# Earlier sorting of x's rows, y's parts made by blocks and halves, and block numbers loaded later on VectorE

## What is computed

```python
h = hybrid_mixer(x, ...)                       # ends with merged @ w_out
x = layer_norm(DEEPNORM_ALPHA * x + h, ln1_w, ln1_b)
# hier_moe: pick one of 4 groups, then the top 2 of its 8 experts for every token
g_sel = argmax(x @ router_group_w + b);  p_group = softmax(...)[g_sel]
top_logit, top_local = lax.top_k(e_logits of that group, 2)
weight = p_group * softmax(top_logit)
order = argsort(expert ids)                    # 512 (token, expert) rows, sorted by expert
hid = silu(xb @ w_gate[e]) * (xb @ w_up[e])    # per expert, 1024 -> 256
yb = hid @ w_down[e]                           # 256 -> 1024
y = zeros.at[token].add(yb * weight)
x = layer_norm(DEEPNORM_ALPHA * x + y, ln2_w, ln2_b)
```

## Time and profile before

| | us |
|---|---|
| median of 3 runs | 1702.05 (1702.04 to 1709.67) |
| profiled execution, its own time | 1701.53 |
| its span in the trace | 1700.3 |
| TensorE products busy | 1543.8 (91%) |
| VectorE busy | 1016.6 (60%) |
| ScalarE busy | 789.8 (46%) |
| all DMA, mean | 183 GB/s |

### The profile page before, as it was taken

How to read it: one execution, slowest core, us unless ns; L and a number is a source line. 1 busy time by engine, 2 the same in 40 slices (tenths; PEclk the granted TensorE clock), 3 DMA queues, 4 the chain that set the end, 5 groups by cost and what they waited for, 6 DMA issues and landing times. The chain is left out here.

```text
span 1700.3 us, 22867 instructions
## 1 busy us (share of the span) xinstructions
PE 1543.8 (91%) x9455; PEld 1304.7 (77%) x9455; DVE 1016.6 (60%) x1264; ACT 789.8 (46%) x1143; POOL 236.5 (14%) x337
## 2 busy tenths in 40 slices
PE   4988899999988899998989898999979899999996
PEld 4977789998977789997987786677868766666664
DVE  6668676666664664445464445773333666666666
ACT  3554565455464565444532312223201476666662
POOL 6530100001340000002880002200002000000000
PEclk9998899999998899999999998799879999999998
DMA  9945278686570165554442131102204289999982
GB/s 347 306 180 199 82 254 290 229 276 207 192 245 25 43 206 199 184 186 140 127 146 75 32 105 50 50 26 87 87 26 169 84 338 340 339 348 343 342 306 89
DMA packets 134589, 310.39 MB, mean 183 GB/s; under 512 B 6239, under 2 KB 99766, under 8 KB 114902
## 3 DMA queue, kind: packets, MB, share of 16 engines
q1 hardware_dynamic: 130326, 299.18, 50.1%
q0 software_dynamic: 3584, 8.71, 2.0%
q10 hardware_dynamic: 576, 1.05, 0.2%
HBM read 307.87 MB, written 1.05 MB: 182 GB/s over the span
## 5 line engine op out<-in xcount | busy, mean ns | idle before, releaser
L338 DVE TENSOR_TENSOR mlp_weights_lo<-weights,mlp_weights_hi 128x2048 fp32r<-128x2048 f32 x64 | 146.4, 2291 | 67.2 <-ACT mlp_weights_hi L328 66.3
L3637 DVE TENSOR_TENSOR expert_pair_lo<-weights,expert_pair_hi 128x2048 fp32r<-128x2048 f32 x53 | 119.8, 2290 | 64.1 <-ACT expert_pair_hi L3628 64.1
L262 PE MATMUL bank<-mlp_in_hi,mlp_weights_hi 128*128 128x256 f32 x512 | 145.0, 283 | 3.1 <-DVE mlp_in_lo L722 3.1
L328 ACT ACTIVATE mlp_weights_hi<-weights 128x2048 fp32r<-128x2048 f32 x64 | 121.9, 1908 | 54.7 <-issue 44.8
L264 PE MATMUL bank<-mlp_in_hi,mlp_weights_lo 128*128 128x256 f32 x512 | 144.9, 283 | 0.0
L263 PE MATMUL bank<-mlp_in_lo,mlp_weights_hi 128*128 128x256 f32 x512 | 144.9, 283 | 0.0
L262 PE MATMUL bank<-expert_pair_hi,x_block_hi 128*128 128x512 f32 x280 | 113.9, 407 | 1.9 <-issue 1.9
L264 PE MATMUL bank<-expert_pair_hi,x_block_lo 128*128 128x512 f32 x280 | 110.3, 394 | 0.0
L263 PE MATMUL bank<-expert_pair_lo,x_block_hi 128*128 128x512 f32 x280 | 110.1, 393 | 0.0
L2185 PE MATMUL bank<-hT,weights 128*128 128x256 f32 x384 | 97.6, 412 | 6.2 <-ACT s_gates L2206 5.2
L262 PEld LDWEIGHTS bank<-mlp_in_hi,mlp_weights_hi 128*128 128x128 f32 x512 | 98.2, 192 | 4.5 <-issue 3.5
(11 more groups left out here) (757 smaller groups left out, 3976.7 us busy)
## 6 DMA issues: line engine op xcount, KB each, us to landing
weights<-in_w_ada SPq DMA_DIRECT2D x48, 1024.0 KB, 5.2
weights<-in_w_in SPq DMA_DIRECT2D x45, 1024.0 KB, 5.4
weights<-in_expert_w_gate SPq DMA_DIRECT2D x35, 1024.0 KB, 4.9
weights<-in_w_up SPq DMA_DIRECT2D x32, 1024.0 KB, 5.5
weights<-in_w_down SPq DMA_DIRECT2D x32, 1024.0 KB, 5.2
weights<-in_expert_w_up SPq DMA_DIRECT2D x18, 1024.0 KB, 6.1
weights<-in_expert_w_down SPq DMA_DIRECT2D x18, 1024.0 KB, 6.8
expert_raw<-in_expert_w_up SPq DMA_DIRECT2D x17, 1024.0 KB, 6.1
```

The lines of the kernel that those rows point to most:

```text
L262: pe.e.matmul(out, lhsT[0], rhs[0], start=start, stop=False)
L328: act.e.activation(self.of(n)[0], ring.view(name), ACT.Copy).then_inc(*act.mark(*self.key, "high", n))
L338: dve.e.tensor_tensor(lo, ring.view(name), hi.bitcast(F32), SUB).then_inc(*dve.mark(*self.key, "low", n))
L3637: dve.e.tensor_tensor(pair[1][:, :, part], expert_raw(s, kind, n), pair[0][:, :, part].bitcast(F32), SUB).then_inc(*dve.mark("expert", "lo ...
```

## The change

The following edits are made, all from the second block's output projection on.

- The buffers of the experts' weights are numbered anew, so that gate and up of expert 0 take the two buffers outside the ring. SyncE issues these two loads once the branch stages are over, ahead of its wait for the ring's last pieces; the other four first loads follow that wait, as before.
- The high and low parts of expert 0's weights are made at the start of the tail, ahead of layer norm 1, where they stood behind the second Exp on ScalarE and behind the slot weights on VectorE.
- The low part of x's rows of t = 1 is made before VectorE waits for the logits.
- TensorE makes the gathers as soon as slots are there, with the transposes of slots between gather 3 and 4 into banks 5 and 6 (`slot_banks`), and the slot weights last. The fillers shrink from 34 to 18 and from 15 to 4.
- ScalarE loads Silu's table with a dummy and the block numbers into its registers before the first copy of a gather; VectorE works on the slot weights after the gathers, and loads its block numbers after the low parts of pair 1.
- For pair 1 ScalarE makes the weights' high parts before the copy of the x block.
- In the last rounds the parts of blocks 0 and 1 are made in pair 33's round and those of block 2 in pair 34's, each in halves of 512 columns; block 3 follows the last sum. The final products run by token tile and half, with the blocks inside.

The diff, cut to its core:

```diff
@@ route_tensor @@
-    keep_going(c, pe, c.banks[7], 34)
+    keep_going(c, pe, c.banks[7], 18)
     yield from pe.wait_ge("slots")
-    yield from pe.wait_ge("token weights")
     slots = s.slots.bitcast(F32)
-    bank = yield from banks.take(pe, "slot weights")
...
-    ins.then_inc(*pe.mark("slot weights"))
     for t in range(TT):
         yield from pe.wait_ge("x rows low", t)
     for k in range(KT):
+        if k == 4:
+            for b0 in range(0, BLOCKS, 2):
+                bank = yield from c.slot_banks.take(pe, "slot T", b0)
...
+                ins.then_inc(*pe.mark("slot T", b0))
         bank = yield from banks.take(pe, "gather", k)
...
-    for b0 in range(0, BLOCKS, 2):
-        bank = yield from banks.take(pe, "slot T", b0)
...
-    keep_going(c, pe, c.banks[7], 15)
+    yield from pe.wait_ge("token weights")
+    bank = yield from banks.take(pe, "slot weights")
...
+    ins.then_inc(*pe.mark("slot weights"))
+    keep_going(c, pe, c.banks[7], 4)
@@ route_scalar @@
-    yield from expert_high(c, s, 0)
+    act.e.activation(s.warm, c.ones[:, 0:1], ACT.Silu).then_inc(*act.mark())
+    yield from act.wait_ge("blocks")
+    values = load_blocks(act, s)
     for k in range(KT):
         yield from act.wait_ge("gather", k)
         act.e.activation(s.x_sorted[0][:, k, :, :], four(banks.of("gather", k)), ACT.Copy).then_inc(*act.mark("sorted high", k))
-    for b0 in range(0, BLOCKS, 2):
-        yield from act.wait_ge("slot T", b0)
...
+        if k == 3:
+            for b0 in range(0, BLOCKS, 2):
+                yield from act.wait_ge("slot T", b0)
...
+    return values
@@ route_vector @@
     yield from dve.wait_ge("route constants")
+    yield from x_rows_vector(c, s, 1)
     yield from dve.wait_ge("logits")
...
     dve.e.tensor_tensor(s.both, s.hot[0], s.hot[1], ADD).then_inc(*dve.mark("pairs"))
-    yield from x_rows_vector(c, s, 1)
     yield from places_vector(c, s)
...
     dve.e.tensor_tensor(s.both, s.hot[0], s.hot[1], ADD).then_inc(*dve.mark("token weights"))
-    yield from slot_weights_vector(c, s)
-    yield from expert_low(c, s, 0)
     for k in range(KT):
         yield from dve.wait_ge("sorted high", k)
...
     dve.also("x sorted")
+    yield from slot_weights_vector(c, s)
@@ expert_slot @@
-    return 3 * (n % 2) + KINDS.index(kind)
+    return (3 * (n % 2) + KINDS.index(kind) + 4) % 6
@@ expert_loads_sync @@
-    for name, _ in ring.order[-RING:]:
-        yield from sp.wait_ge("used", *name)
...
-    for kinds, n in (("gate", "up"), 0), (("gate", "up"), 1), (("down",), 0), (("down",), 1):
-        for kind in kinds:
-            yield from load(kind, n)
+    for name in ("join", *BRANCHES):
+        for engine in c.stages[name].lanes:
+            yield from sp.wait_ge("over", name, "second", engine)
+    for kind in ("gate", "up"):
+        yield from load(kind, 0)
+    for name, _ in ring.order[-RING:]:
+        yield from sp.wait_ge("used", *name)
+    for kind, n in ("gate", 1), ("up", 1), ("down", 0), ("down", 1):
+        yield from load(kind, n)
@@ expert_high @@
     elif n:
-        yield from act.wait_ge("slot T", BLOCKS - 2)
+        yield from act.wait_ge("slot weights")
@@ experts_tensor, after the last pair @@
-    for b in range(BLOCKS):
-        yield from pe.wait_ge("y low", b)
-        for t in range(TT):
-            for half in range(2):
+    for t in range(TT):
+        for half in range(2):
+            for b in range(BLOCKS):
+                yield from pe.wait_ge("y low", b, half)
                 for part in range(2):
...
-                if b == BLOCKS - 1:
-                    ins.then_inc(*pe.mark("y tokens", t, half))
+            ins.then_inc(*pe.mark("y tokens", t, half))
@@ experts_scalar @@
-def experts_scalar(c, s):
+def experts_scalar(c, s, values):
     act = c.moe.act
-    yield from act.wait_ge("blocks")
-    values = load_blocks(act, s)
     yield from act.wait_ge("x sorted")
     yield from x_block_scalar(c, s, values, 0)
...
+        if n < 0:
+            yield from expert_high(c, s, n + 2)
         if n + 2 < PAIRS:
             yield from x_block_scalar(c, s, values, n + 2)
...
-        if n + 2 < PAIRS:
+        if 0 <= n < PAIRS - 2:
             yield from expert_high(c, s, n + 2)
+        if n == PAIRS - 2:
+            yield from y_high_scalar(c, s, 0)
+            yield from y_high_scalar(c, s, 1)
...
         if n == PAIRS - 1:
+            yield from y_high_scalar(c, s, 2)
             act.e.activation(s.warm, c.ones[:, 0:1], ACT.Sqrt).then_inc(*act.mark())
-            for b in range(BLOCKS):
-                yield from act.wait_ge("expert", "added", EXPERTS - 1 + b)
-                act.e.activation(s.y_pair[0][:, b, :], s.y_sorted[:, b, :], ACT.Copy).then_inc(*act.mark("y high", b))
+            yield from y_high_scalar(c, s, 3)
+
+def y_high_scalar(c, s, b):
+    act = c.moe.act
+    for half, part in enumerate(HALVES):
+        yield from act.wait_ge("expert", "added", EXPERTS - 1 + b, half)
+        act.e.activation(s.y_pair[0][:, b, part], s.y_sorted[:, b, part], ACT.Copy).then_inc(*act.mark("y high", b, half))
@@ experts_vector @@
     yield from dve.wait_ge("blocks")
-    values = load_blocks(dve, s)
+    values = None
...
             yield from expert_low(c, s, n + 2)
-    for b in range(BLOCKS):
-        if b == BLOCKS - 1:
-            yield from add_expert(c, s, values, PAIRS - 1)
-        yield from dve.wait_ge("y high", b)
...
+        if n < 0:
+            values = load_blocks(dve, s)
+        if n == PAIRS - 2:
+            yield from y_low_vector(c, s, 0)
+            yield from y_low_vector(c, s, 1)
+    yield from y_low_vector(c, s, 2)
+    yield from add_expert(c, s, values, PAIRS - 1)
+    yield from y_low_vector(c, s, 3)
@@ second_block_scalar @@
     act = c.tail.act
+    yield from expert_high(c, s, 0)
     for t in range(TT):
         yield from rsqrt_scalar(act, s.t_small[:, 0, t, 2:3], "ln1", t)
@@ second_block_vector @@
     dve = c.tail.dve
+    yield from expert_low(c, s, 0)
     yield from dve.wait_ge("landed", "last")
@@ make_stages @@
+    c.slot_banks = Banks(c, 5, 6)
```

More of the change, by code:

```diff
@@ L3368, in route_tensor @@
     ins.then_inc(*pe.mark("places"))
-    keep_going(c, pe, c.banks[7], 34)
+    keep_going(c, pe, c.banks[7], 18)
     yield from pe.wait_ge("slots")
-    yield from pe.wait_ge("token weights")
     slots = s.slots.bitcast(F32)
-    bank = yield from banks.take(pe, "slot weights")
-    for b in range(BLOCKS):
-        for t in range(TT):
-            ins = pe.e.matmul(bank[:, b * 32:(b + 1) * 32], slots[:, t, b * P:(b + 1) * P], s.both[:, t, :], start=t == 0, stop=t == TT - 1)
-    ins.then_inc(*pe.mark("slot weights"))
     for t in range(TT):
@@ L3386, in route_tensor @@
         ins.then_inc(*pe.mark("gather", k))
-    for b0 in range(0, BLOCKS, 2):
-        bank = yield from banks.take(pe, "slot T", b0)
-        for b in (b0, b0 + 1):
-            for t in range(TT):
-                n = (b - b0) * TT + t
-                ins = pe.e.transpose(bank[:, n * P:(n + 1) * P], slots[:, t, b * P:(b + 1) * P], c.identity)
-        ins.then_inc(*pe.mark("slot T", b0))
-    keep_going(c, pe, c.banks[7], 15)
+    yield from pe.wait_ge("token weights")
+    bank = yield from banks.take(pe, "slot weights")
+    for b in range(BLOCKS):
+        for t in range(TT):
+            ins = pe.e.matmul(bank[:, b * 32:(b + 1) * 32], slots[:, t, b * P:(b + 1) * P], s.both[:, t, :], start=t == 0, stop=t == TT - 1)
+    ins.then_inc(*pe.mark("slot weights"))
+    keep_going(c, pe, c.banks[7], 4)
 def x_rows_scalar(c, s, t):
```

23 lines of the change are left out of this document (16 added, 7 removed).

## The result

The changed kernel took 1689.18 us (median of 4 runs, 1685.05 to 1695.95), the kernel before 1704.58 (4 runs, 1702.04 to 1709.67). So it is faster by about 1.1%, where 1.0% was forecast. The median lies 4 us above the forecast of 1685.2. It is outside the forecast's own band (1683 to 1687.5) and inside the wider range that counts the first rival (1682.5 to 1690.5). The profiled execution took 1695.95, its span is 1694.7: only 5.6 us under the span of before, while the median fell by 15.4. That gap is the first thing to be explained.

The account below looks back on a forecast made before the run. TensorE bounds the expert loop, DMA second, so gains lie only before the first product and behind the last. 11.9 + 4.7 = 16.6 us off 1701.53 gives 1684.9, median 1685.2, within 1683 to 1687.5, or 1682.5 to 1690.5 with the first rival.

Parts of the forecast that it names:

- the first rival: Same change, but TensorE's clock falls in other places: gain 11 to 13 us, 1689 to 1691; chance 0.25.
- Expert 0 made early: Ahead of layer norm 1: loads land in median 6.0 us, 4.32 us of cover; cost nothing, up to 3 lost.
- Routing: Logits to slots: x's low part of t = 1 moves into VectorE's idle time, slots ready 0.42 us earlier.
- Sorting: Slots to product 0: early gathers; product 0 at 1341.7 against 1352.78, 11.1 us gained, 2.31 of it ScalarE's register load.
- Pair 1: Product 0 to product 1: product 1 at 1349.5 to 1349.6 against 1361.53; gain so far 11.9, 11.3 if clock falls.
- 2.35 plus 0.7: that sets hidden 0, 1 us late: First pair: VectorE's register load from 1345.7 plus moves ends at 1348.8, behind Silu 0 at 1347.8, delaying hidden 0.
- The register price: Skill's 200 ns per register gives 6.4 us for 32; hidden 0 at about 1352.8, gain smaller by 4 us.
- The end: Last down product to second sum of layer norm 2: 7.6 us instead of 12.3, gain 4.7, bounds 3.0 to 5.0.
- Fewer falls: Under the first rival: idle TensorE pieces under 1.2 us speak for fewer clock falls; cut fillers speak against.
- The second rival: Most front gain missing: ScalarE's register load or expert 0's parts on the path; gain 8.4, 1693; chance 0.09.
- The third: Expert loop becomes DMA's: at 9.9 us a pair or more, 34 pairs cost over 24 us, over 1709; chance 0.03.
- The fourth rival: Sorting still waits for token weights, early gathers gain TensorE nothing else; gain 13.3, 1688.4; chance 0.03.

Follow-up runs that it names:

- e4_expert0_late: Changed kernel with expert 0's high and low parts made late again, its two early loads kept: 1697.96 us.
- e10_x_block_first: Changed kernel with ScalarE's old order in the first round, x block of pair 1 ahead of its high parts: 1694.21 us.
- e1_end_only: Kernel before with only the end changed (y's parts by blocks and halves, last products by tile and half): 1709.01 us.
- e9_act_registers_late: Changed kernel with ScalarE's block numbers loaded behind its last copy of a gather, as before the change: 1692.73 us.
- e6_old_fillers: Changed kernel with the fillers' old counts, 34 and 15: 1693.88 us.
- e3_registers_first: Changed kernel with VectorE's block numbers loaded ahead of the low parts of pair 1 again: 1693.47 us.
- e5: Changed kernel without the two fillers (18 behind the places, 4 behind the slot weights): 1687.28 us.
- e8: Changed kernel with TensorE waiting for the token weights ahead of the gathers, as before the change: 1701.99 us.
- e0_after_again: Changed kernel unaltered, profiled and timed again: median 1690.58 us, ratio 0.989 against the kernel before.

## Why the prediction held, point by point

- **Expert 0 made early: nothing lost, right, but by less than was said.** The step that failed is the landing: it took the median of 6.0 us for both loads and had them there at 7 us; the second landed 11.4 behind its issue, between that median and the bound of 14.8 that was set beside it. The low parts ended 3.5 us later than forecast, and the 4.32 us of cover went down to 0.96. GpSimd's loads came 5.3 us later (e4_expert0_late), but the low parts ended later still, so that cost nothing more.
- **Routing.** The forecast gain of 0.42 is there: from logits to slots 12.65 us before and 12.2 in nine profiles with the changed front. The changed kernel's own profile shows 13.2, and so do e4_expert0_late, e10_x_block_first and e1_end_only with the old code. All four have a stretch of 13.7 us at 1.2 GHz over the logits, in which 22 fillers (7.92 us in the changed kernel's profile) outlast VectorE's choice of experts by 1.3 us. This term was not in the sum at all: projection to slots took between 52.5 and 55.3 us in these 14 profiles, by where the clock was down.
- **Sorting: 13.6 forecast, 13.80 measured**, with the handoffs in the forecast order: gather 4 behind the first low, then TensorE's pace, then the x block. The first low came when it was forecast, but the forecast put it on the token weights alone, and ScalarE's register load and first copy end with them and set it by 0.2 us (e9_act_registers_late). The parts undone one by one: expert 0's parts 4.2, and 2.7 with the clock; gathers 5.07; ScalarE's registers 1.28. Their sum is 13.3 and not 10.43, so they are not independent. The slot weights' place behind the gathers was not undone by itself. The forecast's 2.31 for the registers was too high by 1.0: in the earlier trace rows the load began 0.4 us ahead of the end of the last low, since copies of slots' transposes stood before it, and in e9_act_registers_late 1.3 us ahead.
- **Pair 1: forecast 7.85 us from product 0 to product 1, and 8.5 if the clock falls; measured 7.43 and 8.57.** Five profiles with this code had the clock up over product 0 (7.42 to 7.43, and 7.03 in e6_old_fillers), five had it down (8.43 to 8.58). Against 8.75 before, the gain is 1.32 in the first case and 0.17 in the second. Before, the clock fell over product 0 too, but hidden 0 started at 1360.81, when the last low ended (1360.89), and Silu 0 had ended at 1360.58: by these rows the 8.75 would stand, or nearly, with the clock up (an estimate; no run shows it). The step "2.35 plus 0.7: that sets hidden 0, 1 us late" was right in kind and too large: the load began at 1356.6, 0.5 us ahead of the start of the last low, where the forecast had it begin with that low, and hidden 0 came 0.4 us late. e6_old_fillers, where the load is over in time, shows the same 0.40. At the head of the stage the load costs 0.71 more (e3_registers_first). ScalarE's new order, which the forecast had in its times but never priced, is worth 1.97.
- **The register price.** 2.35 us for 32 registers is 73 ns each, and ScalarE's 2.12 is 66. The Trainium skill, "Runtime: NRT & Kernel Launch" (Instruction fetch mechanics), gives about 200 ns; it speaks of registers loaded from HBM, and these block numbers lie in SBUF. The 4 us that the prediction worked out from that figure appear in no run.
- **The end: 7.6 forecast, 7.68 to 7.69 measured** in all eleven profiles that have the new parts and the new order. The split was not forecast: three quarters lie in the order of the products.
- **Rivals.** The first, a clock that falls elsewhere, is what happened, and more widely than it was put. It was priced at 1.7 us for one fall in the gathers or product 0: a fall over product 0 cost 1.0 to 1.15, as 0.4 of it hides the register load, and a fall over product 1 cost 1.5 (loops of 314.3). The large part came before the change's first instruction. "Fewer falls" is in part borne out: both profiles with the old front had the clock down over slot weights or gathers and over product 0, while with the changed front it was down over the gathers only where an experiment let TensorE idle (e4, e5, e8); over product 0 or 1 it still fell in 7 of 12. The second rival did not happen: layer norm 1 did not slip and the first low came on time. The third neither: the loop is 312.7 to 312.8 us in every profile in which the clock stayed up over product 1. The fourth rival is answered: without the early gathers 5.07 us go.
- **The number.** In the two profiles compared 16.4 us were gained behind slots, and 15.2 in e0_after_again, where the clock fell over product 0. The forecast had 16.2 there and 0.42 in routing, 16.6 together. The median fell by 15.4. The forecast time started from a median of 1702.05 over three runs, and the kernel before gave 1704.58, 1707.32 and 1712.52 in later sets; the base was a low one. The sum was right to half a microsecond stage by stage, while the absolute time came out where the first rival had put it (1689 to 1691), for another reason than the one it gave: not by a smaller gain at layer norm 1 or the gathers.

## What to carry to other kernels

Measure a change of one per cent between marks of its own (end of one named step to start of another) and not by the total: here stretches repeated to 0.1 us while totals moved by 8. When all parts of a result are done before the last one, order the last products so that one output tile is finished at a time, since that alone was worth 3.6 us. Price a load or filler whose cost is "hidden" at its worst landing and at both clocks: in this kernel one cover came within 1 us of its end, and the other, over VectorE's register load, ran out by 0.4 us where the clock stayed up over product 0. When the profile names a releaser that had ended some time before, look at the sequencer's own instructions as well.

## What the runs showed of the hardware

- The sequencer of VectorE begins a register load (TENSOR_LOAD) while its engine still works and with one more instruction waiting to start: at 1356.6, where the last low runs from 1357.1 to 1359.36, and 0.5 us ahead of that low in the ten other profiles with the load in this place. Four others began within 0.1 us of the start of the last instruction ahead of them (1347.3 and 1347.6 in the earlier trace rows, 1348.0 in e3_registers_first, 1343.6 on ScalarE in e9_act_registers_late). The next instruction waits for the load and its moves, about 3.2 us on VectorE: hidden 0 started 0.05 us behind the last move.
- TensorE's clock fell to 1.2 GHz in idle pieces of 4.54, 5.43 and 5.79 us; but also over product 0 behind 1.04 us of idle time, after 16 small products and 4 fillers, in one profile of the changed kernel and not in the other.
- Two loads of 1 MB issued just ahead of six loads on GpSimd's queue (two of 512 KB, one of 128 KB, three of 16 KB or less) delayed the last of those by 5.2 to 5.5 us in the twelve profiles that have them.
